# First tile of the recurrent stage: every product from the input before its root, roots applied to the results, the split input rewritten afterwards

## What is computed

```python
def _rmsnorm(x, g):
    return x * lax.rsqrt(jnp.mean(x * x, axis=-1, keepdims=True) + RMS_EPS) * g

x = x + gt_m * (jnp.square(jax.nn.relu(h @ w_fc1)) @ w_fc2)   # first block's MLP
x = rmsnorm(x, g_final)                                       # "final", kept as the residual
h = _rmsnorm(x, norm_mix_g)                                   # "mix2", input of the recurrent stage
proj = h @ w_in                          # rkv (3 x 1024), glu (2 x 1024), gates (2 x 1024)
rkv  = rkv + (_token_shift(rkv) - rkv) * mu_rkv
dh = _token_shift(h) - h
xw, xa, xg = h + dh * mu_lora[0], h + dh * mu_lora[1], h + dh * mu_lora[2]
w_log = -softplus(-(w0 + tanh(xw @ w1) @ w2)) - 0.5 ; a = sigmoid(a0 + (xa @ a1) @ a2)
g = sigmoid(xg @ g1) @ g2
...                                      # recurrence over 512 steps, in chunks of 64, by head
u = glu_in[..., :D] * sigmoid(glu_in[..., D:])                # gated unit
u = conv(u, conv_w, width 31) + conv_b                        # causal, by channel
```

## Time and profile before

| | us |
|---|---|
| median of 3 runs | 2163.51 |
| lowest, highest | 2160.09, 2170.83 |
| the profiled execution, its own time | 2164.68 |
| its span, first to last instruction | 2162.9 |
| PE busy in the span | 2061.9 |
| DVE, ACT, POOL busy | 1095.3, 788.7, 817.8 |
| mean granted TensorE clock (1 is full speed) | 0.978 |

### The profile page before, as it was taken

One profiled execution on the slowest core, in us unless ns is written; L12 is line 12 of the kernel. 1 busy time (PEld: TensorE's weight loads), 2 busy tenths in 40 slices (PEclk: granted clock), 3 DMA queues, 4 the chain that ended last, 5 costly groups with the idle time before them and its releaser, 6 DMA issues.

```text
span 2162.9 us, 36064 instructions
## 1 busy us (share of the span) xinstructions
PE 2061.9 (95%) x14896; PEld 1627.3 (75%) x14896; DVE 1095.3 (51%) x1754; ACT 788.7 (36%) x1300; POOL 817.8 (38%) x457
## 2 busy tenths in 40 slices
PE   5989989999999999989999999999999998999998
PEld 4866657887788888767777777777777887888886
DVE  6334553243743242637778767776613466524322
ACT  3446654223332232433333333434234333323322
POOL 5324454443444444442233233223233443444442
PEclk9989999999999999989999999999999999999999
DMA  8420013532523333231111111111132432333332
GB/s 318 172 72 21 12 48 110 192 88 78 174 90 97 98 98 98 86 109 33 38 41 48 41 38 48 39 42 31 54 114 68 137 98 78 88 98 98 98 98 68
DMA packets 53041, 186.89 MB, mean 86 GB/s; under 512 B 6032, under 2 KB 7184, under 8 KB 52624
## 3 DMA queue, kind: packets, MB, share of 16 engines
q1 hardware_dynamic: 49104, 174.49, 25.8%
q10 hardware_dynamic: 3776, 10.09, 1.3%
HBM read 178.27 MB, written 6.29 MB: 85 GB/s over the span
## 4 chain that ended last, share of the span: by engine, by line
PE 83%; DVE 6%; ACT 4%; POOL 3%; issue 2%; DMA 1%; DVEq 0%; SPq 0%; ACTq 0%; POOLq 0%
PE psum L882 22%; PE psum L883 20%; PE psum L884 20%; PE psum L1325 2%; POOL wlo L763 2%; PE psum L1320 2%; PE psum L1309 2%; PE psum L1021 2%; PE psum L1042 1%; PE psum L1027 1%; PE psum L1267 1%; ACT whi L1450 1%; DVE sq_sum L1871 1%; PE psum L1299 1%; PE psum L950 1%
## 5 line engine op out<-in xcount | busy, mean ns | idle before, releaser
L763 POOL TENSOR_TENSOR wlo<-raw,whi 128x1024 fp32r<-128x1024 f32 x262 | 630.6, 2408 | 1099.3 <-ACT whi L1450 1099.3
L882 PE MATMUL psum<-ah,whi 128*128 128x512 f32 x1256 | 525.2, 418 | 28.7 <-POOL wlo L763 11.1
L883 PE MATMUL psum<-ah,whi 128*128 128x512 f32 x1256 | 498.8, 397 | 0.0
L884 PE MATMUL psum<-ah,wlo 128*128 128x512 f32 x1256 | 497.3, 396 | 0.0
L1450 ACT ACTIVATE whi<-raw 128x1024 fp32r<-128x1024 f32 x262 | 275.7, 1053 | 310.7 <-PE psum L884 295.2
L882 PEld LDWEIGHTS psum<-ah,whi 128*128 128x128 f32 x1256 | 240.4, 191 | 102.5 <-issue 17.7
L884 PEld LDWEIGHTS psum<-ah,wlo 128*128 128x128 f32 x1256 | 240.8, 192 | 52.9
L883 PEld LDWEIGHTS psum<-ah,whi 128*128 128x128 f32 x1256 | 241.2, 192 | 41.6 <-issue 0.2
L882 PE MATMUL psum<-hidden,whi 128*128 128x512 f32 x536 | 209.8, 391 | 0.1
L2207 DVE SCALAR_TENSOR_TENSOR x<-upad,vec,x 128x512 f32<-128x512 f32 x240 | 206.7, 861 | 5.9
L883 PE MATMUL psum<-hidden,whi 128*128 128x512 f32 x536 | 209.4, 391 | 0.0
(11 more groups left out here) (363 smaller groups left out, 2935.0 us busy)
## 6 DMA issues: line engine op xcount, KB each, us to landing
raw<-in_w SPq DMA_DIRECT2D x300, 512.0 KB, 3.6
raw_first<-in_w SPq DMA_DIRECT2D x14, 512.0 KB, 9.4
raw_ck<-in_w SPq DMA_DIRECT2D x8, 512.0 KB, 7.3
x<-in_x SPq DMA_DIRECT2D x4, 512.0 KB, 6.0
x_kept<-x ACTq DMA_DIRECT2D x1, 2048.0 KB, 9.7
ao_kept<-ao ACTq DMA_DIRECT2D x8, 256.0 KB, 2.0
aof<-ao_kept ACTq DMA_DIRECT2D x1, 2048.0 KB, 10.9
x<-x_kept ACTq DMA_DIRECT2D x1, 2048.0 KB, 8.1
```

The lines of the kernel that those rows point to most:

```text
L763: pool.tensor_tensor(lo_weight(place(s)), raw_of(SPLITS[s]), hi_weight(place(s)).bitcast(F32), ALU.subtract).then_inc(lo_done, 1)
L882: pe.matmul(dst, wh, h_, start=first, stop=False)
L883: pe.matmul(dst, wh, l_, start=False, stop=False)
L884: return pe.matmul(dst, wl, h_, start=False, stop=last)
```

## The change

The first tile's list is written anew. All nine full products of it are now made from the input without its root, and each result is multiplied by the root on its way out of PSUM. `ah` is rewritten with the rooted input only after the last of the nine, and the first product that reads it is `rkv 1 1`. The order of the nine becomes rkv 0 1, rkv 0 0, lora 0 1, lora 0 0, glu 0 1, glu 0 0, lora 1 1, lora 1 0, rkv 0 2; before it was rkv 0 1, rkv 0 0, lora 0 1, lora 0 0, lora 1 1, lora 1 0, rkv 0 2, glu 0 1, glu 0 0. The sums of squares stand between the first and the second product, three spreads between the second and the third. Two spreads are copied by DVE from PSUM into SBUF: `root_both` (for the banks) and `root_again` (for `norm2`, which now starts from the finished x). Nine taps of the convolution move from the recurrence of tile 0 into the first tile. The last input tile's high part and its weights are made ahead of the last squares, its low part by POOL.

```diff
 def first_tile():
-    v, g1, g0 = (parts(what, 1) for what in (("rkv", 0, 2), ("glu", 0, 1), ("glu", 0, 0)))
-    k, r = parts(("rkv", 0, 1), KT), parts(("rkv", 0, 0), KT)
-    normed = [("norm2", i) for i in range(KT)]
+    ks, r, v, g1, g0 = (parts(what, 1) for what in (("rkv", 0, 1), ("rkv", 0, 0), ("rkv", 0, 2), ("glu", 0, 1), ("glu", 0, 0)))
     last0, own0, last1, own1 = (parts(("lora", i, half), 1) for i in range(2) for half in (1, 0))
-    return ([("scale", 0, 1)] + k[:-1] + r[:1] + k[-1:] + r[1:4] + [("factor", 1)] + normed[:2] + [("mix", 0, 1)] + normed[2:5] + r[4:]
-            + normed[5:] + [("factor", 0), ("mix", 0, 0), ("scale", 0, 0)] + last0 + [("scale", 1, 1)] + own0
-            + [("xn", 0), ("scale", 1, 0), ("hidden", 0)] + last1 + [("xput", 0)] + [("lw2", 0), ("la2", 0)] + own1 + [("scan", 0), ("hidden", 1), ("kk", 0)]
-            + v + [("lg2", 0), ("kkss", 0), ("kkinv", 0), ("mix", 0, 2)] + g1 + [("kkb", 0)] + g0 + [("bonus", 0), ("at", 0), ("re", 0)])
+    return ([("scale", 0, 1)] + ks + [("sums", 0)] + r + [("scale", 0, 0), ("spreads", 0)] + last0 + [("scale", 1, 1), ("factor", 1), ("mix", 0, 1)]
+            + [("factor", 0), ("mix", 0, 0)] + own0 + [("scale", 1, 0), ("lput", 0)] + [("xn", k) for k in range(4)] + g1 + [("hidden", 0)]
+            + [("xn", k) for k in range(4, KT)] + [("xput", 0), ("lw2", 0), ("la2", 0), ("gput", 0)] + g0 + [("scan", 0)] + last1
+            + [("kk", 0), ("uput", 0), ("conv", 0, 2), ("lput", 1), ("kkss", 0)] + own1 + [("conv", 0, 2), ("kkinv", 0), ("conv", 0, 3), ("kkb", 0)]
+            + v + [("at", 0), ("re", 0), ("hidden", 1), ("conv", 0, 2), ("norm2", 0), ("norm2", 1), ("factor", 2), ("mix", 0, 2), ("lg2", 0)]
+            + [("bonus", 0), ("norm2", 2)])
+FIRST_TAPS = (0, 0, 2, 2, 1, 0, 2, 2, 4, 0, 2, 2, 1, 2, 0, 2)
...
+        normed = [] if j else [("norm2", k) for k in range(3, KT)]
...
+            got += normed[:2]
+            del normed[:2]
...
-        elif name[0] in ("rkv", "glu", "gate2", "lora"):
+        elif name[0] in ("rkv", "glu", "gate2"):
...
+        root_both, root_again = sq[:, 1, :], sq_sum[:, 1, :]
...
+                if k == KT - 1:
+                    weights_ahead(SPLIT_AT["rkv", 0, 0])
+                    high(("early2", k), ah[:, 0, k, :])
                 square("final", k, x[:, k, :])
                 square("mix2", k, x[:, k, :], scale=vcol("g_final", k))
...
-            dve.wait_ge(const_loaded["rw"], 16)
...
                 elif kind == "norm2":
+                    if j == 0:
+                        wait_emptied(dve, ("glu", 0, 0))
+                        dve.wait_ge(xn_ready, KT)
+                        wait_emptied(dve, ("rb", "again"))
+                    if j == 2:
+                        wait_filled(dve, ("bonus", 0))
-                    dve.scalar_tensor_tensor(slot(("mix2", j)), x[:, j, :], gains2[:, j:j + 1], bank(("rb", "mix2")),
+                    dve.scalar_tensor_tensor(slot(("mix2", j)), x[:, j, :] if j else rp[:, :], vcol("norm_mix_g_2", j), root_again,
                                              ALU.mult, ALU.mult).then_inc(pre_split, 1)
...
                 elif kind == "norm2":
-                    if j < KT - 1:
-                        act.wait_ge(early_used, j + 1)
-                    else:
-                        wait_filled(act, ("rkv", 0, 0))
+                    wait_filled(act, ("rkv", 0, 2))
                     high(("mix2", j), ah[:, 0, j, :])
```

## The result

The changed kernel takes 2150.26 us (median of 6 runs, 2148.51 to 2156.01), the kernel before in the same session 2165.96 us (6 runs, 2160.09 to 2173.30). The ratio is 0.9925, with a 95% interval from 0.9905 to 0.9944: some 12 to 21 us are gained, 15.7 us between the medians. The forecast was 2147.5 us, with a range of 2139 to 2157. It was reckoned as a gain of 16.0 us on the 2163.51 us of the first three runs of the kernel before; the three later ones lifted that median by 2.5 us, so the gain comes out at 15.7 us while the time itself lies 2.8 us above the forecast.

A forecast was written before the change was run, and what follows sets the result against it. The prediction took PE to bound the kernel. Gains of 19.8 us less costs of 3.8 made 16.0 us, taking the median from 2163.51 to 2147.5 us, with a range of 2139 to 2157.

The forecast's parts named there:

- (b): Product lora 0 1: it reads an input long ready instead of waiting for POOL's rewriting; gain 8.8 us.
- (c): Product behind lora 0 1: its first 12 matmuls no longer run at half clock; gain 2.4 us.
- (d): Product at 955.13 us: the wait for late weights and the low clock behind it go; gain 4.9 us.
- term (a): Sums of squares: four steps moved ahead cover the wait for squares, low clock left as before; gain 1.0 us.
- (e): First tile's end: kkb ahead of a full product covers the waits, gain 2.7 us; late `re` costs 1.5.
- (g): Entry to the recurrence: clock recovers but VectorE comes late; net cost 0.5 us, between gain 3 and cost 5.
- (h): Inside tile 0: norm2 of tiles 3 to 7 races with rkv 1 1; cost 1.0 us, between 0 and 3.
- Rival 4: Rewriting runs behind tile 1's product, 5 us for each of five input tiles; 4 us slower, 2168 us, chance 0.06.
- 1 (all covers hold): Rival: no wait at re, clock stays up, entry as in tile 1, norm2 in time; gain 24.4, chance 0.20.
- 2 (VectorE and POOL become the bound there): Rival at the entry: VectorE late by 6 us, the clock falls again; gain 8.5, time 2155 us, chance 0.17.
- 3 (a weight late once): Rival: one weight wait over 2 us, then half clock; gain 11 to 12, 2152 us; chance within the forecast's 0.53.
- 5: Rival: the time lost at the border reappears in tile 0's recurrence; no change, 2163 us, chance 0.04.

The follow-up runs named there:

- e2: Changed kernel with `hidden(1)` ahead of `at`, and the entry's last two taps and norm2 0 to 2 moved behind the recurrence's first steps (iy0); 2152.76 us.
- e12: Changed kernel with the same work, the entry's steps reordered to fill VectorE's gaps and norm2 2 behind the first mb; 2154.49 us.
- e6: Changed kernel's unrooted input and sums position, but the products, kkss, kkb, lg2 and taps in the order of the kernel before; 2165.87 us.
- e5: Changed kernel with the sums back between the fourth and fifth of the eight steps of rkv 0 1; 2153.10 us.
- e10: Changed kernel with the rewriting of input tiles 3 to 7 done for one column of 512, the rest left out; 2149.79 us.
- e8: Changed kernel with, on ScalarE alone, the emptying of lg2's bank into `gate` moved ahead of two high parts and a copy; 2151.49 us.
- e3: Changed kernel with none of the nine taps ahead of the recurrence, all done inside the first tile; 2155.39 us.
- e7: Changed kernel with norm2 and the first tile's taps (all but the first) by one-SBUF-input instructions, root and accumulation left out; 2146.51 us.
- e11: Changed kernel with the rewriting of input tiles 3 to 7 cut to one column and the nine taps back inside the first tile; 2144.47 us.
- e13: Changed kernel with norm2 and first-tile taps by one-SBUF-input instructions over 511 columns; root, accumulation and last column left out; 2147.41 us.
- e4: Changed kernel with norm2 of all eight input tiles computed without the root, by an instruction with one SBUF input; 2149.52 us.

## Why the prediction was right, point by point

**The nine products** were to give 19.8 less 1.5 (`re` late) and 0.8 (one spread more), 17.5 us; they gave 19.76. The kernel before loses 10.77 us there in the waits of the earlier trace rows, the changed one 1.48. The product that was fed by POOL gives 4.0 (9.58 us of running for 5.57), the low clock at 925 and 955 gives 2.4 and 3.0, as (b), (c) and (d) had it. The rest are sizes. The sums took 3.50 us, not 4.58, at full clock, and the low clock behind them is 0.8 us cheaper (11 matmuls in 3.5 us for 12 in 4.5); term (a) took both as unchanged, and they are most of what E gave beyond the forecast. `re` was not late, 1.5 us too many on the bill, but only since a new wait of 1.24 us for `lh`, not on the bill, stood ahead: in e2 and e12, without that wait, 0.49 and 1.38 us for `re` appear. The walk gave its lateness rightly and missed its cover.

**What (b) to (e) were put down to does not hold.** Ahead of e6 I had laid 11.4 us to the input without its root, and 5.6 to the order. Of e6, which has the input without the order, 1.2 us are left in the stretch. One step of the prediction that holds in the new order alone is "the lora exits are DVE and ACT work under products; their price is nothing as long as DVE has room": there two products more give that room. In the old order the same steps and the `xn` end at 926, and since the next product's bank is the one that the last `xn` reads, they cost PE 4.36 us and a stretch at the lower level. The other is that the rewriting costs 1.0 us in the tile, which needs the taps out of it; in e6 they are in, and R is 5.3 us longer.

**The entry (g)** was sized at 0.5 and cost 1.45, inside its bounds; e5 and e10, with the same entry, would have made it 0.7. It is the difference of two larger things, as (g) had it: 1.4 us came back by the clock (PE busy 12.79 us at 0.60 before, 11.42 at 0.76 now), and 2.8 us of waits were paid. The prediction's "12.8 us at 0.74 clock" was misread: 0.74 is the row of 980 to 990 us, the stretch itself had 0.60. And its twelve steps at 0.7 and 0.2 us are 8.6, not 8.8; neither moves the sum. VectorE was to be 3 to 4 us late at the first mb's bank: it was 3.8. The reason, GpSimd's instructions in the way of VectorE's, stands in the rows at 951 to 960. The reading "waits first for re, then for a bank that DVE or ACT frees late" is half right: `re` was not waited for, the bank was `gate`'s, and e8 shows that it was VectorE's lateness in ScalarE's name.

**The race (h)** was sized at 1.0 and cost 0.85, 0.90 by e10, little more than R's spread of 0.7: right in number, for half of the reason. My working compared POOL's 2.5 us with PE's 2.5 us. Rival 4's price, "5 us for each against the 0.7 that PE wants", is real in part, with another engine as its likely cause: where the taps are in the tile too, the five rewritings cost 8.9 us, 1.8 for each. What kept the cost at 1 was the diff's new table of taps, and of that the prediction says only "tile 0 has nine taps fewer". What it lacks is a pair of terms, some 8 us of loss and 8 us of gain; that they cancel was luck. With all nine taps in the tile (e3) the stretch gives 10.8 us (161.66 less 150.86), of which 1.5 us are E's chance, so the forecast of 16.0 would have been 4 to 5 us too high.

**The rivals and the signs.** 1 (all covers hold) fell at the entry. 2 (VectorE and POOL become the bound there) has the right mechanism at the wrong size: 1.45 for 5. 4 (slower by the rewriting) did not come; even in e3 the five rewritings cost 8.9 us, not 21. 3 (a weight late once) did not come: the longest wait for a weight or an input among the nine is 0.24 us. 5 fell: 17.46 us arrive at the second tile. Two of the signs named for a wrong prediction came true beside a right forecast: the clock fell at the entry (0.63 and 0.68 in the rows above), and tile 0 took 78.98 us up to the second tile's first mb, more than the 77 that it took before. Neither could serve as a sign, since the clock had fallen there before too (0.60), and (g) and (h) themselves put 1.5 us on the 76.7.

**From the sum to the time.** 17.46 us in the stretch, 14.80 in the spans, 15.7 in the medians: the difference is the wander of the untouched parts, up to 6.5 us ahead of the border and 5.8 us behind the second tile's start over the fourteen executions, which no step of the prediction allowed for by name. That 15.7 comes so near to 16.0 is partly luck: the stretch itself gave 1.5 us more than forecast (2.3 more in E, 0.8 more paid at the entry and in the tile), and the wander of the rest took that surplus back.

## What to carry to other kernels

Count moved work at both ends: the same nine taps cost the first tile 8.5 us or 0.6, by what else stood in the stretch, and two loads that hide alone need not hide together, so walk the helper engine once with all that the change puts on it. Credit a removed dependency only with the order that gives its helpers time. Where a wait names one engine, ask whether that engine was itself waiting: three reorderings that cured the named wait left the sum within 0.7 us.

## What the hardware showed that I had not expected

- A copy of eight columns, 0.17 us alone (0.16 in e6), took 1.92 us beside a weight split of POOL and ended with it: a tiny instruction was held up as long as a full one.
- One SBUF input is no protection: the instruction that takes 485 ns alone took 946 to 955 ns in the mean over tiles 1 to 7 and up to 1891 ns beside POOL, with 512 and with 511 columns.
- The clock fell at the entry with few waits: in e12 1.38 and 0.25 us of idle time were followed by 0.50 and 0.61 of full clock, while in e3, e7, e11 and e13, which wait three times there and just ahead, for 0.17 to 1.25 us each, it stayed at 1.00. What decides between them these runs do not show.
- The same code around the sums had a stretch of 7 to 9 slow matmuls in ten of the twelve executions that have the sums in the new place, and of 13 and 14 in the other two (e4, e3), worth 1.5 to 1.6 us.
